# Second expert stage of a transformer kernel: two halves of 1408 inner columns in place of five units of 512 and a tail

## The reference, cut to what matters

```python
def _moe_swiglu(u, w_router, w_gate, w_up, w_down):
    ...
    top_logits, top_idx = lax.top_k(logits, TOP_K)
    top_w = jax.nn.softmax(top_logits, axis=-1).astype(u.dtype)
    ...
    xs = xt[tok]
    h = jax.nn.silu(lax.ragged_dot(xs, w_gate, group_sizes)) * lax.ragged_dot(xs, w_up, group_sizes)
    ys = lax.ragged_dot(h, w_down, group_sizes) * top_w.reshape(-1)[order][:, None]
    out = jax.ops.segment_sum(ys, tok, num_segments=n_tok)
```

## Time and profile before

| | |
|---|---|
| median of 3 runs | 2123.36 us (2122.05 to 2128.01) |
| span of the profiled execution | 2122.7 us (the trace holds no other time of it) |
| second expert stage, first product on PE to its last expert's transposes | 1379.44 to 2100.91 us: 721.47 us |
| TensorE busy in the whole span | 1999.8 us (94%) |
| DVE, ACT busy in the whole span | 568.9 us (27%), 201.7 us (10%) |
| bytes through the main DMA queue | 647.41 MB |

### The profile page before, as it was taken

How to read it: one execution, slowest core, us unless ns; L and a number is a source line. 1 busy time by engine, 2 the same in 40 slices (tenths; PEclk the granted TensorE clock), 3 DMA queues, 4 the chain that set the end, 5 groups by cost and what they waited for, 6 DMA issues and landing times.

```text
span 2122.7 us, 68259 instructions
## 1 busy us (share of the span) xinstructions
PE 1999.8 (94%) x31257; PEld 1605.4 (76%) x31257; DVE 568.9 (27%) x1312; ACT 201.7 (10%) x332; POOL 19.2 (1%) x69
## 2 busy tenths in 40 slices
PE   6999989999999989999999999889899999989996
PEld 4777567778777757748767577589898999989895
DVE  4203342222223241263323523411011110101104
ACT  2112020000000001000000110110101101010100
POOL 1000000000000000000000000000000000000000
PEclk9999999999999999999999999899999999999998
DMA  9797659999999995327667533099999999999992
GB/s 352 233 359 289 238 204 377 422 424 420 421 422 425 421 380 218 120 85 293 221 219 281 194 119 119 20 368 372 395 380 395 382 380 395 383 394 370 388 389 91
DMA packets 245814, 655.82 MB, mean 309 GB/s; under 512 B 17364, under 2 KB 38260, under 8 KB 237556
## 3 DMA queue, kind: packets, MB, share of 16 engines
q1 hardware_dynamic: 237216, 647.41, 80.2%
q0 software_dynamic: 1456, 5.24, 0.7%
q10 hardware_dynamic: 7076, 2.20, 0.4%
HBM read 653.76 MB, written 1.05 MB: 308 GB/s over the span
## 4 chain that ended last, share of the span: by engine, by line
PE 81%; DMA 11%; DVE 4%; SPq 2%; issue 1%; DVEq 0%; ACT 0%
PE ps L1628 79%; DMA ring<-in_moe_w_up_dram 11%; PE ps L1636 2%; SPq L429 2%; DMA ring<-in_w_ada_dram 1%; DVE stat L1001 0%; DVE arena L1201 0%; DVE x L1108 0%; DVE tok L905 0%; DVE tok L1107 0%; DVE newton L898 0%; DVE hT L984 0%; DVE x L995 0%; DVE hT L918 0%; DVE arena L1073 0%
## 5 line engine op out<-in xcount | busy, mean ns | idle before, releaser
L1628 PE MATMUL ps<-arena,ring 128*64 128x80 f32 (+2 forms) x25216 | 882.5, 232 | 50.6 <-DMA ring<-in_moe_w_up_dram 46.2
L1628 PEld LDWEIGHTS ps<-arena,ring 128*64 128x64 f32 (+1 forms) x25216 | 867.6, 139 | 73.4 <-DMA ring<-in_moe_w_up_dram 50.2
L1628 PE MATMUL ps<-hT,ring 128*128 128x256 f32 (+1 forms) x1680 | 360.2, 386 | 4.1 <-DVE stat L922 2.2
L1628 PEld LDWEIGHTS ps<-hT,ring 128*128 128x128 f32 (+1 forms) x1680 | 309.3, 189 | 54.1 <-issue 8.2
L1628 PE MATMUL ps<-ring,arena 128*64 128x512 f32 (+1 forms) x880 | 273.8, 595 | 1.5 <-DVE stat L1536 1.1
L1628 PE MATMUL ps<-arena 128*128 128x128 f32 (+7 forms) x1296 | 230.1, 345 | 10.4 <-DVE arena L1473 5.6
L1628 PEld LDWEIGHTS ps<-ring,arena 128*64 128x64 f32 (+1 forms) x880 | 104.7, 159 | 150.7 <-issue 147.0
L1628 PEld LDWEIGHTS ps<-arena 128*128 128x128 f32 (+4 forms) x1296 | 158.1, 192 | 63.1 <-issue 42.7
L1358 DVE TENSOR_TENSOR arena<-arena,ps 128x160 f32<-128x160 f32 x88 | 28.3, 321 | 528.9 <-PE ps L1628 528.9
L1628 PE MATMUL ps<-ring,hT 128*128 128x512 f32 (+2 forms) x256 | 87.6, 500 | 0.0
L1260 DVE TENSOR_TENSOR x<-x,ps 128x512 f32<-128x512 f32 x104 | 71.6, 688 | 32.8 <-PE ps L1628 32.4
(11 more groups left out here) (321 smaller groups left out, 737.4 us busy)
## 6 DMA issues: line engine op xcount, KB each, us to landing
ring<-in_moe_w_gate_dram SPq DMA_DIRECT2D x160, 512.0 KB, 10.0
ring<-in_moe_w_up_dram SPq DMA_DIRECT2D x160, 512.0 KB, 7.3
ring<-in_moe_w_down_dram SPq DMA_DIRECT2D x160, 512.0 KB, 10.3
ring<-in_w_gate_dram SPq DMA_DIRECT2D x32, 2048.0 KB, 14.9
ring<-in_w_up_dram SPq DMA_DIRECT2D x32, 2048.0 KB, 14.3
ring<-in_w_down_dram SPq DMA_DIRECT2D x32, 2048.0 KB, 12.6
ring<-in_w_in_dram SPq DMA_DIRECT2D x19, 2048.0 KB, 13.5
ring<-in_w_ada_dram SPq DMA_DIRECT2D x12, 2048.0 KB, 16.9
```

Of the source, the lines that this page charges most:

```text
L1628: ins = pe.matmul(*args, **kw)
```

## The change

The inner columns are cut into two halves of `FH` = 1408, 11 tiles of 128 each. The ring is seen as two regions of 8 x 1408 floats per partition (5.8 MB each), and an expert as a stream of six blocks: gate of half 0, up of half 0, gate of half 1, down of half 0, up of half 1, down of half 1, in regions 0, 1, 0, 1, 0, 1. Down of half 0 is thus used one block behind. Gate and up are loaded by row blocks of 128 x 1408 (720 KB, rows of 5.6 KB), down by row blocks of 128 x 1024 (512 KB): 32 + 22 = 54 single transfers an expert, each with a semaphore of its own for its arrival and a wait of its own for the space.

```diff
+STREAM = ((GATE, 0), (UP, 0), (GATE, 1), (DOWN, 0), (UP, 1), (DOWN, 1))
+REGION = (0, 1, 0, 1, 0, 1)
...
+            for (block, j, region, lo, hi), need in zip(pieces, needs):
+                if need >= 0:
+                    sp.wait_ge(held_free, need + 1)
+                else:
+                    sp.wait_ge(ring_free, MOE2_SEQ - SLOTS + 1 + (region * BLOCK + hi - 1) // SLOT)
+                load_piece(0, block, j, region)
             with sp.Fori(1, NE2) as e:
...
-                load_unit(e, 0, lambda j: (unit_free, e * (FREES * UNITS) + (j + 1 - FREES)))
-                load_tail(e, [(tail_free, e * 2 - 1), (tail_free, e * 2), (PH[2]["y_full"], e)])
-                more_units(e)
+                for (block, j, region, lo, hi), need in zip(pieces, needs):
+                    if need == -1:
+                        sp.wait_ge(PH[2]["y_full"], e)
+                    else:
+                        sp.wait_ge(held_free, e * last + (need + 1 + (need < 0)))
+                    load_piece(e, block, j, region)
```

```diff
-                with pe.Fori(0, NE2) as i:
-                    with pe.Fori(0, UNITS) as u:
-                        unit(i, u)
-                    unit_ready([tail_full["gate"]], i)
...
+                def rows_in(region, i, nth, per, bank, done):
+                    for k in range(KD):
+                        piece_in(held_full[region][k], i, nth, per)
+                        for f in range(TH):
+                            at = f % BANK_TILES * cap
+                            for c in range(2):
+                                last = mm(ps[c * HALF:(c + 1) * HALF, bank + f // BANK_TILES, at:at + cap],
+                                          held_rows[region][:, k, f * P + c * HALF:f * P + (c + 1) * HALF], xT[:, k, 0:cap],
+                                          start=(k == 0 and f % BANK_TILES == 0), stop=(k == KD - 1),
+                                          skip_group_check=True)
...
+                def expert(i, first):
+                    pe.wait_ge(q["side_free"], 2 if first else side_op(i, 0))
+                    gate(i, 0)
+                    if not first:
+                        turned(i)
+                    up(i, 0)
+                    if not first:
+                        combine_two(i, 0)
+                    gate(i, 1)
+                    if not first:
+                        combine_two(i, 1)
+                    down(i, 0)
+                    weights(i)
+                    up(i, 1)
+                    dispatch_to(i)
+                    down(i, 1)
+
...
+                expert(0, True)
+                with pe.Fori(1, NE2) as i:
+                    expert(i, False)
```

```diff
-                    dve.wait_ge(q["y_free"], i * 2 + 2)
-                    dve.memset(ps[:, 4:6, 0:4 * cap], 0.0).then_inc(q["y_free"], 1)
...
+                def product(i, u):
+                    dve.wait_ge(q["silu_done"], i * 2 + (u + 1))
+                    dve.wait_ge(q["up_full"], i * 2 + (u + 1))
+                    for b, (at, n) in enumerate(bank_spans(cap)):
+                        dve.tensor_tensor(hid2[:, u, at:at + n], hid2[:, u, at:at + n], ps[:, UP_BANK + b, 0:n], ALU.mult)\
+                           .then_inc(q["hid_ready"], 1)
```

More of the change, by code:

```diff
@@ L81, in __init__, with stream_pieces, stream_needs, touches @@
         self.sem, self.n = sem, 0
+def stream_pieces():
+    out = []
+    for block, (kind, _) in enumerate(STREAM):
+        n, width = (TH, D) if kind == DOWN else (KD, FH)
+        out += [(block, j, REGION[block], j * width, (j + 1) * width) for j in range(n)]
+    return out
+def stream_needs():
+    own = stream_pieces()
+    n = len(own)
+    needs = []
+    for i, (_, _, region, lo, hi) in enumerate(own):
+        def touches(k):
+            _, _, r, a, b = own[k % n]
+            return r == region and a < hi and lo < b
+        needs.append(max(k for k in range(i - n, i) if touches(k)))
+    return needs
 class Ring:
+    FIRST = 2
     def __init__(self):
@@ L243, in build @@
         ring_free = sem("ring_free")
[L245 to L249, removed]
+        held_full = [[sem(f"held{r}_full{k}") for k in range(KD)] for r in range(2)]
+        down_full = [sem(f"down_full{f}") for f in range(TH)]
+        held_free = sem("held_free")
         v_full, v_free, a_full, a_free = sem("v_full"), sem("v_free"), sem("a_full"), sem("a_free")
@@ L415, in _ @@
                     load_chunk(11)
-            assert r.seq == MOE2_SEQ
+            assert r.seq == MOE2_SEQ and (MOE2_SEQ + r.FIRST) % SLOTS == 0
             wg, wu, wd = a["moe_w_gate_2"][0], a["moe_w_up_2"][0], a["moe_w_down_2"][0]
[L419 to L452, removed]
-            with sp.Fori(1, NE2) as e:
-                load_unit(e, 0, lambda j: (unit_free, e * (FREES * UNITS) + (j + 1 - FREES)))
-                load_tail(e, [(tail_free, e * 2 - 1), (tail_free, e * 2), (PH[2]["y_full"], e)])
-                more_units(e)
+            pieces, needs = stream_pieces(), stream_needs()
@@ new lines, in downs_of @@
+                def downs_of(i, u):
+                    pe.wait_ge(q["hid_ready"], i * per + (u + 1) * len(dense_spans))
+                    for f in range(TH):
+                        pe.wait_ge(down_full[f], i * 32 + 16 * (u + 1))
+                        for t in range(TT):
+                            for half in range(2):
+                                last = mm(ps[:, 2 * t + half, :], dense2[:, u, f * T + t * P:f * T + (t + 1) * P],
+                                          held_down[:, f, half * CH:(half + 1) * CH],
+                                          start=(u == 0 and f == 0), stop=(u == 1 and f == TH - 1))
+                        if u == 0 or f < TH - 1:
+                            last.then_inc(held_free, 1)
+                    if u:
+                        last.then_inc(q["y_full"], 1)
@@ new lines, in turned, with combine_two @@
+                def turned(i):
+                    pe.wait_ge(q["y_free"], i)
+                    for half in range(2):
+                        pe.wait_ge(q["side_free"], side_op(i, 0))
+                        for j in range(4):
+                            last = tr(ps[0:cap, SIDE2[half], j * P:(j + 1) * P], yT[:, 4 * half + j, :], ident[:, :])
+                        last.then_inc(q["side_full"], 1)
+                def combine_two(i, t):
+                    pe.wait_ge(q["side_free"], side_op(i, 2 + 2 * t))
+                    for half in range(2):
+                        pe.matmul(ps[:, SIDE2[2 + 2 * t + half], :], pickT[0:cap, t, :],
+                                  y_slot[0:cap, half * CH:(half + 1) * CH], start=True, stop=True)\
+                          .then_inc(q["side_full"], 1)
@@ L2206, in second_slots @@
+                pe.wait_ge(q["pick_ready"], 1)
+                for c in range(2):
+                    tokens_out(SIDE2[7 + c], c, cap).then_inc(q["side_full"], 1)
+                expert(0, True)
+                with pe.Fori(1, NE2) as i:
+                    expert(i, False)
                 turned(NE2)
[L2207 to L2209 removed]
+                combine_two(NE2, 0)
```

305 lines of the change are left out of this document (162 added, 143 removed).

## The result

| | before | changed |
|---|---|---|
| time, median | 2123.8 us (2122.1 to 2128.0, 4 runs) | 2222.1 us (2217.3 to 2226.7, 4 runs) |
| ratio | | 1.0465 [1.0438, 1.0492] |
| profiled span | 2122.7 us | 2222.2 us |
| second expert stage | 721.5 us | 823.3 us |

The changed kernel is 4.7% slower. The forecast was 2150 us, range 2066 to 2215: the direction is right and the time is 7 us above the range. Of the 99.5 us between the spans 99.0 are the stage's: it begins 2.8 us sooner and lasts 101.8 us longer.

The account below looks back on a forecast made before the run. DMA packets were taken as the bound, with PE waiting for `moe_w_up`. PE's work 668.4, crossings 45 and branches 36 made the stage 749.4 us against 721.5; with -0.8 at the end, 2150 us, range 2066 to 2215.

Parts of the forecast that it names:

- PE's work, 668.4 us: Second expert stage: PE's busy time, 673.2 us before less 4.8 us for expert 0's empty turn and combine.
- the end, -0.8: End of the kernel: DVE's clearing leaves the path, saving 0.8 us.
- 17 packets an expert, fetched in every one: PE's expert loop: its 2172 pairs fill 17 program packets, not held, each fetched anew in every expert.
- Branch back, 6 x 6 = 36 us: End of PE's expert loop: PE waits for program packets 6 us at each of 6 branches, 36 us in all.
- The data wait goes: Second expert stage: PE's waits for weights nearly vanish, a gain of 53 us.
- my 84 us an expert: Weight supply in the second expert stage: 34.6 MB an expert arrive in 84 us, between 82.2 and 89.6.
- a rate above 400 GB/s by full slices: Sign in the second expert stage: DMA engines move over 400 GB/s by full slices, their share below 1 with gaps.
- Crossings, 14 x 8 x 0.4 = 45 us: Inside expert bodies: 14 packets in each of 8 experts come 0.4 us late, at 4.9 us a packet; 45 us.
- The sum: Second expert stage: 668.4 + 45 + 36 = 749.4 us, against 721.5 us before; chance 0.45.
- The first (no cost): Rival: program fetching costs nothing and PE's work alone bounds the stage, 668.4 us; 2070 us in all; chance 0.25.
- the second (only the branch): Rival: crossings are hidden and only the branch back costs, stage 704.4 us, 2106 us in all; chance 0.09.
- The third: Rival: loaded packet time throughout, 134 us for 112 crossings and 60 us for branches; 2264 us; chance 0.13.

Follow-up runs that it names:

- The table of loads: The changed kernel with weight pieces cut to 128 columns, half, three quarters, or uncut: 2092.4, 2099.9, 2148.0 and 2222.1 us.
- the first experiment: The kernel before with only PE's loop over the 5 units written out, 17 packets of program per expert: 2271.2 us, ratio 1.071.
- the light kernel: The changed kernel with each weight transfer of the second expert stage cut to 128 columns: 2092.4 us, ratio 0.984.
- the thirds: The kernel before, inner loop kept, with three units of seven tiles and a tail of one instead of five of four and a tail of two: 2182.4 us.
- the shifted thirds: Like the thirds, with 80 PE instructions in a never-taken branch ahead of the stage, so the loop lies in 7 packets: 2085.2 us, ratio 0.981.

## Why the prediction came out as it did

*PE's work, 668.4 us; the end, -0.8.* PE was busy for 700.05 us, 31.6 us more than that. Two terms that I had at nothing make up most of it. The clock: in the changed kernel ten stretches of the stage, 61.4 us in all, are at 0.50, and PE is busy for 43.8 us in them; before there were seven, 23.9 us, with PE busy for 23.0. At half the clock that is about 22 us of work lost now and 11 before, so some 10 us more. And each cut run drains: 128 pairs take 4.64 us alone and 4.49 in a long run, 0.15 us x 86 = 13 us. About 8 us of PE's busy time stay unexplained.

*17 packets an expert, fetched in every one.* Right: 107 in 600 us, with a pass of 105 us, is 18 to 19 with those fetched ahead.

*Branch back, 6 x 6 = 36 us.* Right for the stops: the six pairs, as 5.41 + 0.89 above, sum to 36.2 us. That it comes out to the microsecond is luck, since 6 us were a choice between 3.3 and 11.4. And the stops are not the whole price: PE was busy for 30.5 us in the six stretches of low clock that begin in them, another 15 us or so.

*The data wait goes.* Right. Whether the supply would have reached my 84 us an expert is not shown, as PE's stops let the loads keep up at 326 GB/s. I had named a rate above 400 GB/s by full slices as a sign; the highest slice of 1480 to 2080 us has 398.

*Crossings, 14 x 8 x 0.4 = 45 us.* This step failed: the mechanism was there, its size was not. The crossings are 121.8 - 36.2 = 85.6 us in 74 stops, 1.2 us for each stop or 0.76 us on each of the 112, and with their drains (74 x 0.15 us) 97 us. I had put a packet's time at 4.9 us, between 3.3 idle and 5.7 loaded, with the ground that a PE that stops leaves the queue short. Measured are 5.8 us. The table of loads shows why a value between the ends was wrong: time does not grow in proportion to the load, but stays at what PE needs up to 62% and rises steeply from 80%, and the stage stayed at 88%. My ground failed too. In PE's stop at the branch, 1570.5 to 1575.9 us, the data queue's share was 98.7%: the loads run on at full load through the stop. That this holds for the shorter stops too, and is why the next packets are late, is my reading; no run separates it.

*The sum.* The stage took 823.3 us, 73.9 more than my 749.4. Of these 41 are the crossings' stops, 13 the drains of all 86 stops, 10 the clock and 2 the idle time that is not after issue; the other 8 are the busy time that stays unexplained.

*The rivals.* The first (no cost) and the second (only the branch) fell with the first experiment; the light kernel shows what they describe, 2092 us. The third had the right time for a packet, 1.2 us over the need, but put it on all 112 crossings, where only 74 stopped PE: 97 us with the drains against its 134. Its 60 us for the branch are too much as well, against 36 us of stops and 15 us of low clock. The Trainium skill's sentence that crossing a page is mostly hidden (Runtime: NRT & Kernel Launch, "Instruction fetch mechanics") holds in this kernel up to a load of 62%, and not at 89%. Its room for 2048 instructions, which is 8 pages of 256, agrees with the two versions of the thirds if one page of the 8 is taken by the fetch ahead; that last part is inferred from the nine packets in each expert. The same section's remark that there are only two such pages at hand disagrees with loops of 7 that ran without one fetch, and the measurement decides.

*What the prediction should have weighed.* That the length of a loop decides, was in it. What it did not do was to ask how the same larger pieces could be had in a loop that is held; the shifted thirds are that answer.

## What to carry to other kernels

Before unrolling a loop on PE, count its instructions in packets of 256, from the border of a packet: here 7 are held, and an eighth costs 97 us in 8 passes, 86 of them in the stops of a stage whose DMA engines are full. Crossing from packet to packet in a straight body cost nothing only while the DMA engines had room (up to 62% here); the branch back cost 24 us even with little traffic. If a loop is a few instructions too long, look first at where it begins; unreached code ahead of it moves it at no cost.

## What the runs showed of the hardware

- Packets of PE's program come the later, the busier the DMA engines are with data: 4.6 us from one to the next at 62% load, 5.1 at 80%, 5.8 at 89%, and 6.2 in the first experiment at 86%, whose gate and up rows are 2 KB. Smaller packets of data did not make it quicker.
- A loop inside a loop is held for itself: the thirds' inner body (5.3 packets) was fetched once per expert, though the outer loop was not held.
- The hint for the branch back brought its target 3.0 us earlier, and the next packet 2.7 us later.
- A stop of PE can bring the low clock with it: in the changed kernel the granted clock fell to 0.50 inside each of the six stops of 5.3 to 5.5 us at the branch, for 6.8 to 10.2 us. In the kernel before, each of the seven such stretches begins at or just behind a data wait of 2.4 us, the second or third in a row.
- Larger rows carried more: in the stretch 1480 to 2080 us the data queue moved 231.30 MB at 103.6% in rows of 2 KB and 226.46 MB at 96.8% in rows of 3.5 KB, 2.233 and 2.339 MB per per cent, 5% more for each busy engine. The changed kernel's rows of 5.6 KB do not continue this over the same stretch: 199.48 MB at 89.4% are 2.231. With the queue full, in the stop at 1570.5 to 1575.9 us, it moved 405 GB/s, where the kernel before moved 386.
